# A gated linear recurrence beside dilated attention: weight pieces at the start, projections between the products of the scan, and a new order of the steps

## What is computed

```python
u = rms_norm(x, norm_w)                      # x: (1, 2048, 1024), float32
proj = einsum('bsd,dc->bsc', u, w_in)        # 4096 columns
hg_q, hg_f, hg_i, hg_z, at_q, at_k, at_v, at_z = split(proj)   # 512 each
# recurrence, 4 heads of 128: f = lb + (1-lb) sigmoid(hg_f), k = 1 - f
#   S_t = diag(f_t) S_{t-1} + outer(k_t, hg_i_t);  o_t = S_t^T silu(hg_q_t)
o_hg = rms_norm_per_head(o_hg) * g * silu(hg_z)
# attention, 8 heads of 64, rope, causal windows (128,1), (512,4), (2048,16)
#   (window, dilation), merged by the softmax of their log-denominators
o_at = o_at * silu(at_z)
y = einsum('bsc,cd->bsd', concatenate([o_hg, o_at]), w_out)
return rms_norm(x + y, final_norm_w)
```

## Time and profile before

| | |
|---|---|
| median of 3 runs | 1338.95 us (1337.79 to 1342.43) |
| the profiled execution | 1334.58 us, span 1332.6 us |
| busy: TensorE, weight loads | 1278.4 us, 1117.6 us |
| busy: VectorE, ScalarE, GpSimd | 708.1, 462.9, 437.8 us |
| transfers | 143.9 MB, mean 108 GB/s |

### The profile page before, as it was taken

The page is one execution under the profiler, slowest core; times in us unless marked ns, Lnnn a source line. Parts: engine busy times, 40 slices in busy tenths (PEclk is TensorE's granted clock), DMA queues, the critical chain, the costliest instruction groups (busy, mean ns, idle before and its releaser), DMA issues.

```text
span 1332.6 us, 23428 instructions
## 1 busy us (share of the span) xinstructions
PE 1278.4 (96%) x8520; PEld 1117.6 (84%) x8520; DVE 708.1 (53%) x1885; ACT 462.9 (35%) x1328; POOL 437.8 (33%) x441
## 2 busy tenths in 40 slices
PE   5999999999999999999999999999999999999997
PEld 5989998989899888989888787888778877878886
DVE  5837773767568557830245534554455456333332
ACT  5721122122112211211355544555454457311111
POOL 5742243334323321330234434443444344102000
PEclk9999999999999999999999999999999999999999
DMA  6520032012202311234256455554555567545431
GB/s 210 165 85 20 33 88 84 21 48 84 79 21 75 88 52 33 84 107 111 55 145 150 118 134 127 152 128 105 144 136 127 142 178 193 171 134 174 142 112 63
DMA packets 121714, 143.89 MB, mean 108 GB/s; under 512 B 20352, under 2 KB 86400, under 8 KB 121600
## 3 DMA queue, kind: packets, MB, share of 16 engines
q1 hardware_dynamic: 119200, 138.46, 37.1%
q10 hardware_dynamic: 2400, 3.93, 1.1%
HBM read 87.56 MB, written 29.62 MB: 88 GB/s over the span
## 4 chain that ended last, share of the span: by engine, by line
PE 70%; DMA 12%; DVE 8%; POOL 3%; issue 2%; SPq 2%; ACT 2%; ACTq 0%; DVEq 0%; POOLq 0%
PE bank L633 9%; PE bank L635 8%; PE bank L634 8%; PE bank L767 4%; PE bank L793 4%; PE bank L794 4%; PE bank L795 4%; PE bank L766 4%; PE bank L765 4%; DMA stage<-in_w_groups 4%; DVE room L1399 2%; PE bank L702 2%; PE bank L861 2%; PE bank L870 2%; PE bank L930 2%
## 5 line engine op out<-in xcount | busy, mean ns | idle before, releaser
L633 PE MATMUL bank<-w_hi,u_hi 128*128 128x256 f32 x768 | 220.9, 288 | 2.6 <-POOL w_lo L1217 2.1
L634 PE MATMUL bank<-w_lo,u_hi 128*128 128x256 f32 x768 | 217.8, 284 | 0.0
L635 PE MATMUL bank<-w_hi,u_lo 128*128 128x256 f32 x768 | 217.8, 284 | 0.0
L1399 DVE TENSOR_TENSOR room<-room 128x256 f32<-128x256 f32 (+6 forms) x386 | 135.6, 398 | 40.3 <-POOL room L1281 36.8
L633 PEld LDWEIGHTS bank<-w_hi,u_hi 128*128 128x128 f32 x768 | 147.8, 192 | 4.8 <-POOL w_lo L1217 2.0
L634 PEld LDWEIGHTS bank<-w_lo,u_hi 128*128 128x128 f32 x768 | 147.9, 193 | 0.2
L635 PEld LDWEIGHTS bank<-w_hi,u_lo 128*128 128x128 f32 x768 | 147.7, 192 | 0.0
L1399 DVE TENSOR_TENSOR t<-bank,tab 128x512 f32<-128x512 f32 x64 | 42.6, 687 | 134.7 <-DMA tab<-in_rope 65.6
L766 PE MATMUL bank<-u_lo,w_hi 128*128 128x512 f32 x256 | 102.2, 399 | 5.9 <-DMA far_v<-values 5.8
L765 PE MATMUL bank<-u_hi,w_hi 128*128 128x512 f32 x256 | 107.7, 421 | 0.0
L633 PE MATMUL bank<-u_hi,w_hi 128*128 128x512 f32 x256 | 101.6, 397 | 4.7 <-ACT room L1064 2.0
(11 more groups left out here) (169 smaller groups left out, 2933.2 us busy)
## 6 DMA issues: line engine op xcount, KB each, us to landing
qd<-turned SPq DMA_DIRECT2D x64, 256.0 KB, 4.7
stage<-in_w_groups SPq DMA_DIRECT2D x44, 256.0 KB, 3.9
room<-in_x SPq DMA_DIRECT2D x16, 512.0 KB, 4.6
values_gates<-vg_tile SPq DMA_DIRECT2D x64, 128.0 KB, 1.7
room<-values_gates SPq DMA_DIRECT2D x16, 512.0 KB, 4.5
tab<-in_rope SPq DMA_DIRECT2D x16, 512.0 KB, 5.8
wide<-mix_weights SPq DMA_DIRECT2D x32, 256.0 KB, 3.9
xr<-in_x SPq DMA_DIRECT2D x16, 512.0 KB, 5.3
```

The source lines that it names most:

```text
L633: nc.tensor.matmul(dst, lhs_hi(k), rhs_hi(k), start=(k == 0), stop=False)
L634: nc.tensor.matmul(dst, lhs_hi(k), rhs_lo(k), start=False, stop=False)
L635: last = nc.tensor.matmul(dst, lhs_lo(k), rhs_hi(k), start=False, stop=(k == KT_N - 1))
L1399: return nc.vector.tensor_tensor(dst, a_, b_, op)
```

## The change

- The start: weight pieces 2 and 3 of group 0 go to `w_raw`, a buffer of their own, and are issued right behind pieces 0 and 1, ahead of x tiles 2 and 3. TensorE waits for each piece where its matmuls begin. Tile 0's high part on ScalarE stands ahead of the square of tile 2, its low part on VectorE ahead of the work on tile 1, and its projection ahead of the transposes of tile 2.
- The recurrence: one list over all units. P runs two blocks ahead, over the border of a unit too. Loads (G, H) and splits (V, W) of weight pieces are steps of their own; tiles are 3, 3, 3, 3 (after four ahead of the first scan), 4, 4, 4, 4 twice, and 2, 3, 6, 5. Values of a block are loaded two blocks ahead. Odd tiles use bank 5 (the states') in place of bank 4, some of the last unit bank 0.
- The scan: behind each level product stand three matmuls of the next query projection, or five of a value tile. The product of level 3 loads 64 columns in place of 128, and VectorE writes the level's operands so that they lie together.
- Attention: SP issues far and near values ahead of the store and of the next weights. `turn_weights` stands behind the second far scores and the matmuls beside them.

```diff
+HG_TILES = ((3, 3, 3, 3), (4, 4, 4, 4), (4, 4, 4, 4), (2, 3, 6, 5))
+def hg_steps():
+    steps = [("N", 0, 0), ("G", 0, 0), ("G", 0, 1), ("P", 0, 0)] + [("V", 0, i) for i in range(2)]
+    steps += [("G", 0, 2), ("G", 0, 3), ("K", 0, 0), ("L", 0, 0), ("P", 0, 1)]
+    steps += [("V", 0, 2), ("V", 0, 3)] + [("T", 0, t) for t in range(4)]
+    for n in range(HG_BLOCKS):
...
+        steps.append(("M", u, b))
+        if n + 1 < HG_BLOCKS:
+            steps += [("K", *divmod(n + 1, BLOCKS)), ("L", *divmod(n + 1, BLOCKS))]
+        if b == 0 and u > 0:
+            steps += [("V", u, 2), ("V", u, 3)]
+        if n + 2 < HG_BLOCKS:
+            steps.append(("P", *divmod(n + 2, BLOCKS)))
+        else:
+            steps += tiles[:2]
+            tiles = tiles[2:]
+        if b == 1:
+            steps += [("H", u, 0), ("H", u, 1)]
+        steps.append(("O", u, b))
+        if b == 1:
+            steps += [("W", u, 0), ("W", u, 1), ("H", u, 2), ("H", u, 3)] + tiles + [("W", u, 2), ("W", u, 3)]
+            tiles = []
+        if b == BLOCKS - 1 and u + 1 < HG_UNITS:
+            steps += [("G", u + 1, 0), ("G", u + 1, 1)] + tiles + [("N", u + 1, 0)]
+            steps += [("V", u + 1, 0), ("V", u + 1, 1), ("G", u + 1, 2), ("G", u + 1, 3)]
+        else:
+            steps += tiles
+        steps.append(("Z", u, b))
...
@@ split_matmuls, phase1_tile @@
+                for k in range(KT_N):
+                    if pieces is not None and k % 2 == 0:
+                        pe.wait_ge(lo_done, pieces + k // 2 + 1)
+                    yield nc.tensor.matmul(dst, lhs_hi(k), rhs_hi(k), start=(k == 0), stop=False)
...
-                if t == 0:
-                    pe.wait_ge(lo_done, U * 8 + 4)
...
@@ prologue on TensorE @@
-                if t + 2 < TILES:
+                if t == 1:
+                    x_transposes(2)
+                if 1 <= t < TILES - 2:
                     x_transposes(t + 2)
                 pe.wait_ge(ulo_done, t + 1)
...
@@ scan_block @@
+                        if l == COMPACT:
+                            last = nc.tensor.matmul(bank[2 + l % 2][0:64, c * 64:(c + 1) * 64], ka[:, c * P:c * P + 64],
+                                                    qa[:, c * P + 64:(c + 1) * P], start=True, stop=True)
...
+                    last.then_inc(lev_mm, 1)
+                    run(itertools.islice(beside, many))
...
+                    if after_it[0] == "P":
+                        scan_block(u, b, queries(*after_it[1:]), 3)
+                    else:
+                        scan_block(u, b, value_tile(*after_it[1:]), 5)
...
@@ VectorE, prologue @@
+                if step == 2:
+                    low_parts(0)
                 if 0 <= t < TILES:
                     dve.wait_ge(xT_done, t + 1)
...
@@ SP, attention @@
-                if v + 1 < AT_UNITS and (g, i) in ((1, 2), (2, 0), (2, 3)):
-                    z = ((1, 2), (2, 0), (2, 3)).index((g, i))
-                    load_unit_piece(unit_pieces(v + 1)[2 * z])
-                    load_unit_piece(unit_pieces(v + 1)[2 * z + 1])
...
-                if i == 2 and n >= 1:
-                    after(comb_done, n)
-                    store_output(n - 1)
                 if T >= 1:
                     after(pv_mm, T)
                     load_far(T)
...
+                if i == 2 and n >= 1:
+                    after(comb_done, n)
+                    store_output(n - 1)
+                if v + 1 < AT_UNITS and (g, i) in ((1, 2), (2, 0), (2, 3)):
...
@@ scores @@
                     far_scores(0)
-                    if j == 1 and n >= 1:
-                        turn_weights(n - 1)
                     far_scores(1)
                 for _ in beside:
                     pass
+                if j == 1 and n >= 1:
+                    turn_weights(n - 1)
```

461 lines of the change are left out of this document (243 added, 218 removed).

## The result

The changed kernel takes 1330.0 us (median of 11 runs, 1326.1 to 1334.6) against 1337.8 for before on the same chip: ratio 0.9941, interval 0.9922 to 0.9960. In a second series, beside other kernels, it was 0.9936 (0.9916 to 0.9956). It is faster by 0.6%, where 24.2 us (1.8%) were forecast, and 1330.0 lies just outside the range of 1304 to 1329. The profiled execution took 1330.0 (span 1328.2) against 1334.58 before, so profile against profile there are 4.6 us to explain.

A forecast was written before the change was run, and what follows sets the result against it. TensorE, busy 96% of the span, was taken as the bound. The terms 1.4 + 10.2 + 7.3 + 0.4 + 4.6 + 0.3 = 24.2 us, off the median of 1338.95, gave 1314.7 us; range 1304 to 1329.

The forecast's parts named there:

- Start: Prologue: tile 0 starts at about 15.1 us, tile 1 at about 23.5 against 24.88; 1.4 us gained, bounds 0 and 4.7.
- The scan itself: Recurrence scans: a covered 0.26 us wait and 0.38 us of smaller weight loads, times 16 scans; 10.2 us gained.
- The waits of the recurrence: Three whole units: all 10.8 us of TensorE's idle time goes, 3.5 of new waits come; 7.3 us gained net.
- A: Rival, recurrence: VectorE's chain takes over, waits 17 us in place of 3.5; gain only 10.7, 1328.2 us; chance 0.15.
- C: Rival, recurrence: VectorE bounds every block with a 30.2 us cycle; slower, 1345.2 us; chance 0.04.
- After the last unit: Last value group: tile 0's 1.61 us wait falls to 0.4, a new 0.8 comes before attention projections; 0.4 net.
- Far values: Attention: issuing far and near values first removes 4.6 of 5.8 us that TensorE waited for far values.
- Mixing-weight transposes: Attention: their later place wins 3.3 us of waits, loses 3.0 to far transposes' waits; 0.3 net, bounds -2 and 3.3.
- Rival D: Whole kernel: waits only change place and eat the smaller loads' gain; within 4 us of before; chance 0.03.

The follow-up runs named there:

- e3: The changed kernel with both attention moves undone (sync queue order and mixing-weight transposes back as before): median 1324.7 us, ratio to before 0.9904.
- e7: The changed kernel with the scan's fourth level product loading 128 weight columns again in place of 64: ratio to before 0.9947.
- e9: The kernel before with only the sync queue's new order in attention (far and near values first): ratio to before 1.0031.
- e10: The kernel before with only the mixing-weight transposes moved behind the second far score: ratio to before 1.0018.
- e8: The kernel before with both attention moves, the sync queue's new order and the mixing-weight transposes' new place: ratio to before 1.0072.

## Why the prediction was wrong

- **Start**, forecast 1.4, measured -0.6 in the profile and -0.4 on average. Tile 1 did start at 23.1 (23.7 to 24.6 in the other seven profiles, with 23.5 forecast). The step that failed is the one that carried that lead to the end of the prologue. The clock explains it in one profile of eight; in e3, where tile 1 ran at full clock and ended 1.0 earlier than before, TensorE waits 0.63, 0.29, 0.65 and 0.64 us for VectorE at 35, 43, 57 and 69 us, where before waits 0.40 and 0.21. The forecast looked at no tile behind tile 1. It took the lead of tile 1 for the lead of the stage, and the average lies below even its lower bound, a gain of nothing.
- **The scan itself**, forecast 10.2, measured 5.3 (16 times 5.91 less 5.58). The loads were mis-sized, at 0.38 a scan: the product got shorter by 0.20, the gap ahead of it longer by 0.10, and e7 shows 0.07 over the recurrence. The guests were counted as if matmuls could be put between others for 0.229 each; they took 0.69 more, of which shorter products gave back 0.55.
- **The waits of the recurrence**, forecast 7.3, measured 9.7: the 10.8 went whole, and new ones were 1.1 (0.70 and, behind the three units, 0.39) and not 3.5. Rivals A and C, with VectorE's chain as the bound, did not come true at all.
- **After the last unit**, forecast 0.4, measured 0.6: the 1.61 became 0.51 (ahead of the attention projections, at 563.16) and 0.52 (in tile 0, at 577.00). The four terms make 15.0 of the 15.8 that were measured up to attention, against 19.3.
- **Far values**, forecast 4.6 of 5.8. This is the step whose failure cost most. The wait went where it was read, and only 2.1 of it net. The prediction put the later weight loads at nothing, "because ScalarE splits them a tile later". That was wrong in two ways. It did not ask which transfer is behind the moved ones: the pieces were set behind a wait of the queue and ahead of the query gather, and 13.4 us of waits for keys and queries came in place of 4.8. And the cover that it named was not there: ScalarE waited 13.0 us for the pieces where it had waited 0.3, and TensorE 2.9 in place of 0.9 for ScalarE. By e9 the new order cost 4 us (interval 1 to 7), where 4.6 were to be won.
- **Mixing-weight transposes**, forecast 0.3, bounds -2 and 3.3: by e10 -2.4, with an interval from nothing to -5, so no error is shown here. Both moves together cost 8.5 by e8; with the 15.0 up to attention that makes a gain of 6.5, where the medians show 7.8.
- Rival D ("nothing") asked for the waits to change place, which is what attention did; the recurrence did not. The upper end of the range was set by A, the wrong mechanism, and no rival was made for the sync queue. That A's 1328.2 lies so near the 1330.0 is luck.

## What to carry to other kernels

When a DMA issue is moved on a queue, write down what stands behind it on that queue and on the other issuing queues, and when each is needed; the transfer that is moved forward is not the one that ends up late. Ask the same of the engine that works on what lands: a split that waits for late data holds up all that stands behind it. Test a doubtful part of a change also by making it alone in the old kernel: there the two moves showed 8.5 us clearly, while taking them out of the new one gave 3 to 4 with overlapping intervals. Guests between small matmuls cost a seam each, so interleaving pays where it covers more than that.

## What the runs showed of the hardware that was not expected

- Loads of 64 weight columns did not start under a running 512-column matmul whose own weights had 128: the loads stood still for 0.36 us, against full overlap for 128-column loads behind such a guest, and 0.07 for 64-column loads behind small matmuls.
- The first 512-column matmul behind a group of small ones took 0.31 to 0.34 to the next start, where later ones took 0.23; the small products behind a guest took 0.81, where they took 0.89 to 0.93 behind each other.
- The same program's profiled attention lasted 496.8 and 508.5 us on one kernel; over twelve runs time went with the mean granted clock (correlation -0.84). The clock fell behind some waits of about 2 us and not behind others of the same length.
